# Latent attention's inputs: latent sums and sine inside the projection, rotations between the query units, keys and values in two loads

## What is computed

```
proj = h @ w_in                                   # 1024 -> 384 + 256 + 64
cq, ckv, k_rope = split(proj, [384, 640])
q  = (rmsnorm(cq, g_q)   @ w_q_up ).reshape(B, S, 8, 128 + 64)
kv = (rmsnorm(ckv, g_kv) @ w_kv_up).reshape(B, S, 8, 128 + 128)
q_rope, k_rope = apply_rope(q_rope, cos, sin), apply_rope(k_rope, cos, sin)
s = (q_nope @ k_nope.T + q_rope @ k_rope.T) * scale      # causal softmax, then @ v
```

## Time and profile before

| | us |
|---|---|
| median of three runs | 3182.15 |
| their lowest and highest | 3175.34 and 3193.03 |
| the profiled execution | 3190.56 |
| its span in the trace | 3188.1 |

### The profile page before, as it was taken

One profiled execution on the slowest core, in us unless ns is written; L12 is line 12 of the kernel. 1 busy time (PEld: TensorE's weight loads), 2 busy tenths in 40 slices (PEclk: granted clock), 3 DMA queues, 4 the chain that ended last, 5 costly groups with the idle time before them and its releaser, 6 DMA issues.

```text
span 3188.1 us, 26936 instructions
## 1 busy us (share of the span) xinstructions
PE 2737.7 (86%) x8901; PEld 1634.9 (51%) x8901; DVE 1407.4 (44%) x3069; ACT 624.7 (20%) x1276; POOL 1870.1 (59%) x1393
## 2 busy tenths in 40 slices
PE   8998998777777777777787999899999858899998
PEld 7644443332233223333233476678877534678877
DVE  6747466666666666666414302431111336221111
ACT  2211212121111111111122111321100213121101
POOL 5205666767776777677758770346554482355653
PEclk9999999989998899999999899899999978899999
DMA  6338999999999999999954341022322340123222
GB/s 194 106 111 326 385 365 377 409 400 409 409 409 389 409 409 409 393 409 409 409 202 146 130 133 53 27 79 94 103 86 94 93 156 14 40 79 105 92 91 81
DMA packets 304627, 720.39 MB, mean 226 GB/s; under 512 B 24916, under 2 KB 162050, under 8 KB 304530
## 3 DMA queue, kind: packets, MB, share of 16 engines
q0 software_dynamic: 157248, 574.69, 46.2%
q1 hardware_dynamic: 134802, 131.93, 12.8%
q10 hardware_dynamic: 12480, 12.58, 1.2%
HBM read 717.02 MB, written 2.10 MB: 226 GB/s over the span
## 4 chain that ended last, share of the span: by engine, by line
PE 58%; POOL 14%; DMA 12%; issue 8%; DVE 5%; ACT 2%; SPq 0%; POOLq 0%; DVEq 0%; ACTq 0%
PE ps L881 11%; PE ps L593 10%; PE ps L585 10%; PE ps L589 10%; POOL arena L1263 8%; DMA arena<-in_expert_u_dram,arena 8%; PE ps L846 3%; POOL work L1263 3%; PE ps L979 2%; PE ps L531 2%; PE ps L542 2%; PE ps L794 2%; DMA arena<-in_expert_v_dram,arena 2%; POOL arena L1209 1%; POOL arena L1206 1%
## 5 line engine op out<-in xcount | busy, mean ns | idle before, releaser
L881 PE MATMUL ps<-arena 128*128 128x512 f32 x1536 | 764.7, 644 | 250.0 <-ACT arena L1575 164.6
L881 PEld LDWEIGHTS ps<-arena 128*128 128x128 f32 x1536 | 304.2, 206 | 690.7 <-issue 556.4
L2172 DVE CUSTOM_DVE_ANT_0 arena<-arena,ps 128x1024 f32<-128x1024 f32 x384 | 467.6, 1219 | 306.1 <-DMA arena<-in_expert_u_dram,arena 297.2
L1263 POOL DMA_INDIRECT arena<-in_expert_v_dram,arena x384 | 361.2, 941 | 190.3 <-PE ps L881 100.7
L1263 POOL DMA_INDIRECT arena<-in_expert_u_dram,arena x384 | 361.9, 942 | 149.7 <-issue 100.2
L1236 POOL TENSOR_SCALAR whi_f<-wring 128x2048 fp32r<-128x2048 f32 (+1 forms) x60 | 125.3, 2088 | 317.0 <-DMA wring<-in_ffn_w_in_dram 191.1
L1240 POOL TENSOR_TENSOR wlo<-wring,whi_f 128x2048 fp32r<-128x2048 f32 (+1 forms) x60 | 302.7, 5044 | 11.1 <-POOL whi_f L1236 11.1
L881 PE MATMUL ps<-work,arena 128*128 128x512 f32 x512 | 240.4, 602 | 27.0 <-DMA work<-in_expert_v_dram,arena 27.0
L589 PE MATMUL ps<-n_hi,wlo 128*128 128x512 f32 x1024 | 258.5, 395 | 0.0
L589 PEld LDWEIGHTS ps<-n_hi,wlo 128*128 128x128 f32 x1024 | 195.1, 191 | 43.1 <-issue 1.1
L2355 DVE TENSOR_TENSOR arena<-ps,arena 128x512 f32 x44 | 30.4, 692 | 406.4 <-PE ps L593 406.4
(11 more groups left out here) (307 smaller groups left out, 3698.1 us busy)
## 6 DMA issues: line engine op xcount, KB each, us to landing
wring<-in_ffn_w_in_dram SPq DMA_DIRECT2D x44, 1024.0 KB, 5.0
arena<-in_ada_w_dram POOLq DMA_DIRECT2D x36, 1024.0 KB, 5.9
wring<-in_ffn_w_out_dram SPq DMA_DIRECT2D x16, 1408.0 KB, 6.2
arena<-in_ada_w_dram ACTq DMA_DIRECT2D x12, 1024.0 KB, 6.0
wring<-in_gla_w_in_dram SPq DMA_DIRECT2D x12, 1024.0 KB, 5.2
wring<-in_w_in_dram SPq DMA_DIRECT2D x9, 1024.0 KB, 5.7
wring<-in_w_q_dram SPq DMA_DIRECT2D x8, 1024.0 KB, 10.4
arena<-in_expert_u_dram,arena POOLq DMA_INDIRECT x384, 9.7
```

The lines of the kernel that those rows point to most:

```text
L881: mm = e.matmul(ps[:, 6 + q, :], diag[:, k, :], slot_of(s)[:, q * 512:(q + 1) * 512], start=(n % HEADS == 0 and k == 0), stop=last)
L1263: e.indirect_dma_start(slot_of(seq), None, table, bass.IndirectOffsetOnAxis(ap=idx_flat[:, n * TOPK + k:n * TOPK + k + 1], axis=0)).then_i ...
L2172: inc(e.tensor_tensor_reduce(slot_of(s), slot_of(s), ps[:, 4:6, :].rearrange("p a k -> p (a k)"), 1.0, 0.0, ALU.mult, ALU.add, dots[:, n % ...
```

## The change

ScalarE takes the squares of the five latent chunks out of PSUM next to each copy, into the free tiles `qn`. TensorE sums the first three behind the second projection unit and the other two behind the third. The sine, with its two table loads, stands on ScalarE behind the fourth chunk. The rotary key tile and the four query tiles are rotated inside the query and key units, one behind the second chunk of each query unit and one behind the third key chunk, in banks 6 and 7; VectorE combines them in the order 4, 0, 1, 2, 3. Keys and values come in two loads of four heads (1024 KB each) in place of eight of 256 KB; each load gives four key chunks and four value chunks, a value chunk now being 128 tokens by four heads' 128 columns, taken as a strided slice of the weights. GpSimd's `ada(3)` waits for `norm_full` 6 instead of 5. The counters of chunks are adjusted (eight units become two).

```diff
@@ SP
-            units(IN["mla_w_kv_up_2"][0], 0, 8, 2)
+            for u in range(2):
+                unit(IN["mla_w_kv_up_2"][0], u * 4 * (NOPE + VDIM), 2, width=4 * (NOPE + VDIM), chunks=8)
@@ TensorE, split_linear
-                    for x in lands:
+                    for i, x in enumerate(lands):
                         one(x)
+                        if i in after:
+                            after[i]()
@@ TensorE, latent attention
-            split_linear("mla_in", 3, whi_m, n_hi, n_lo, act, operand(), lands=(16, 16, 32))
-            squares(3, 4)
-            squares(2, 5)
+            def latent_sums(first, n, bank):
+                for k in range(n):
+                    need("sq_ready", c["sq_ready"].at + 1)
+                    mm = e.matmul(ps[:, bank, :], ones[:], qn[:, first + k, :], start=(k == 0), stop=(k == n - 1))
+                inc(mm, "ms_ready")
+
+            def rotate(i):
+                r = (4, 0, 1, 2, 3)[i]
+                if i >= 2:
+                    need("rope_read", i - 1)
+                mm = e.matmul(ps[:, 6 + i % 2, :], rotm[:], cT6[:, 5, :] if r == 4 else qr[:, r, :], start=True, stop=True)
+                inc(mm, "rot_done")
+
+            split_linear("mla_in", 3, whi_m, n_hi, n_lo, act, operand(), lands=(16, 16, 32),
+                         after={1: lambda: latent_sums(0, 3, 4), 2: lambda: latent_sums(3, 2, 5)})
+            base = 2 * (st["u"] % 2)
             need("norm_full", 5)
-            settle()
             for m in range(4):
                 w = slot(3, width=384, n=64)
                 for j in range(3):
                     e.wait_ge(act.sem, act.value(3))
...
                     inc(mm, "chunk_done")
                     act.add()
+                    if j == 1:
+                        e.wait_ge(act.sem, act.value(2))
+                        rotate(m)
             need("norm_full", 6)
+            for u in range(2):
+                w = slot(2, width=4 * (NOPE + VDIM))
+                for i in range(8):
+                    bank = ps[:, (base + 8 * u + i) % 4, :]
+                    e.wait_ge(act.sem, act.value(3))
+                    for k in range(2):
+                        if i < 4:
+                            at = i * (NOPE + VDIM)
+                            mm = e.matmul(bank, w[:, k, at:at + NOPE], cT6[:, 3 + k, :], start=(k == 0), stop=(k == 1))
+                        else:
+                            t = i - 4
+                            values = w[:, k, :].rearrange("p (h c) -> p h c", c=NOPE + VDIM)[:, :, NOPE:NOPE + VDIM]
+                            mm = e.matmul(bank.rearrange("p (h c) -> p h c", c=VDIM), cT6[:, 3 + k, t * P:(t + 1) * P], values,
+                                          start=(k == 0), stop=(k == 1))
+                    inc(mm, "chunk_done")
+                    act.add()
+                    if u == 0 and i == 2:
+                        e.wait_ge(act.sem, act.value(3))
+                        rotate(4)
             settle()
-            def kv_unit():
...
-            pairs_of(MLA_H, kv_unit, act)
-            settle()
-            for r in range(5):
...
             need("rope_ready", 5)
             settle()
@@ GpSimd
-            e.wait_ge(S["norm_full"], 5)
+            e.wait_ge(S["norm_full"], 6)
             ada(3)
@@ ScalarE
-            units(3, copy_to(cT6))
-            e.wait_ge(evacs.sem, evacs.value())
-            squares([cT6[:, k, :] for k in range(3)])
-            root(384)
-            squares([cT6[:, 3 + k, :] for k in range(2)])
-            root(256, bank=5)
...
+            def latent(i):
+                bank = ps[:, 2 * ((st["u"] + i // 2) % 2) + i % 2, :]
+                done.add()
+                e.wait_ge(done.sem, done.value())
+                if i < 5:
+                    inc(e.activation(qn[:, i, :], bank, ACT.Square), "sq_ready")
+                e.activation(cT6[:, i, :], bank, ACT.Copy).then_inc(evacs.sem, 1)
+                evacs.add()
+
+            for i in range(4):
+                latent(i)
             need("angle_ready", 1)
             inc(e.activation(tri, rtmp, ACT.Sin), "trig_ready")
             roots_next()
+            root(384)
+            latent(4)
+            latent(5)
+            root(256, bank=5)
...
@@ VectorE
-            e.wait_ge(S["act_evac"], st["act"] + 6)
             rms(cT6, cT6, lambda k: col("mla_g_q_2", k), 3)
             rms(cT6[:, 3:5, :], cT6[:, 3:5, :], lambda k: col("mla_g_kv_2", k), 2, bank=5)
-            e.wait_ge(S["act_evac"], st["act"] + 6 + 12 + 16)
             need("trig_ready", 1)
-            for r in range(5):
+            for i, r in enumerate((4, 0, 1, 2, 3)):
                 x = cT6[:, 5, :] if r == 4 else qr[:, r, :]
-                need("rot_done", r + 1)
-                own(e.tensor_tensor(rtmp[:, 0, :], ps[:, 4 + r % 4, :], tri[:, 1, :], ALU.mult), "rope_read")
+                need("rot_done", i + 1)
+                own(e.tensor_tensor(rtmp[:, 0, :], ps[:, 6 + i % 2, :], tri[:, 1, :], ALU.mult), "rope_read")
                 own(e.tensor_tensor(x, x, tri[:, 0, :], ALU.mult))
                 own(e.tensor_tensor(x, x, rtmp[:, 0, :], ALU.add), "rope_ready")
```

More of the change, by code:

```diff
@@ L596, in split_products, with split_linear @@
                         between()
-            def split_linear(name, n, high, hi, lo, evac, ready=None, lands=None):
+            def split_linear(name, n, high, hi, lo, evac, ready=None, lands=None, after=None):
                 settle()
@@ L1060, in _ @@
                     for k in range(3):
-                        mm = e.matmul(ps[:, (3 * m + j) % 4, :], w[:, k, j * P:(j + 1) * P], cT6[:, k, :], start=(k == 0), stop=(k == 2))
+                        mm = e.matmul(ps[:, (base + 3 * m + j) % 4, :], w[:, k, j * P:(j + 1) * P], cT6[:, k, :],
+                                      start=(k == 0), stop=(k == 2))
                     inc(mm, "chunk_done")
                     act.add()
+                    if j == 1:
+                        e.wait_ge(act.sem, act.value(2))
+                        rotate(m)
@@ L1769, in _, with up @@
             roots_next()
+            root(384)
+            latent(4)
+            latent(5)
+            root(256, bank=5)
+            st["u"] += 3
+            base = 2 * (st["u"] % 2)
+            def up(i, dst):
+                done.add()
+                e.wait_ge(done.sem, done.value())
+                e.activation(dst, ps[:, (base + i) % 4, :], ACT.Copy).then_inc(evacs.sem, 1)
+                evacs.add()
+            for m in range(4):
+                for j in range(3):
+                    up(3 * m + j, qr[:, m, :] if j == 2 else qn[:, 2 * m + j, :])
+            for u in range(2):
+                for i in range(8):
+                    up(8 * u + i, kn[:, 4 * u + i, :] if i < 4 else vt[:, i - 4, u * 4 * VDIM:(u + 1) * 4 * VDIM])
+            st["u"] += 4 + 2
             SCALE = float(NOPE + ROPE) ** -0.5
@@ L2438, in _ @@
             low_out(MLA_H - 1)
-            skip(3 + 4 + 8)
+            skip(3 + 4 + 2)
             modulation(3)
-            done.add(4)
+            done.add(16)
             residual(gate=48 + 16)
```

## The result

Eight runs of the changed kernel had a median of 3155.65 us (3153.18 to 3161.43) beside 3186.38 us (3171.22 to 3193.03) for eight runs of the kernel before: ratio 0.9915, with an interval of 0.9896 to 0.9933. It is faster: the ratio puts it at about 27 us, and the two medians lie 30.7 apart. The forecast was 3135; its range, 3116 to 3158, holds the time.

A forecast was written before the change was run, and what follows sets the result against it. TensorE was the bound but stood still in handovers before attention. Scores 44.7 us earlier plus 16.1 on the first head, less 14 of contention, gave 46.8: 3143.8 from the profiled 3190.56, or 3135 against the median 8.4 lower; range 3116 to 3158.

The forecast's parts named there:

- The string in front of attention: Handovers from the last projection unit to the first scores: scores start at 2582.8 instead of 2627.5, 44.7 us earlier.
- nothing between ends 0 and 14: Value chunks in the key and value stage: strided weight slices cost 0 us extra, bounds 0 and 14 us.
- No wait for the two loads: Key and value weights in two 1024 KB loads: 0 us of waiting taken, bounds 0 and 3.
- The 10.9 us for keys and values: Key and value stage: 28.4 us against 39.3, 10.9 gained, nearly all of it the missing DMA waits.
- The stalls: Attention beside GpSimd: stalled scaling of probabilities exposes 2.4 us a head over five heads, 12 us, ends 7 and 25.
- The clock: TensorE in attention: clock dips follow the longest stalls, costing 2 us, ends 0 and 6.
- A sign that the prediction had named for being wrong: Attention: the prediction would be wrong if heads beside GpSimd take over 15 us.
- The first head: First head of attention: with the idle gone the clock stays up, 14.5 us instead of 30.6, 16.1 gained.
- The last head: End of attention: the last head was counted at 9.6 us.
- the contention: Attention beside GpSimd: stalls of 12 us and clock dips of 2 give back 14 us, 7 to 31.
- The one that gave 3152: Rival in attention: VectorE becomes the bound, stalls reach TensorE and dips follow; 31 us given back, gain 30; chance 0.17.
- The slower case: TensorE in attention: clock stays down, 7.9 us more a head, slower from 7.7 half-rate heads on, up to 3210; chance 0.02.

The follow-up runs named there:

- the last experiment: Exponentials left in PSUM and the unread matmul, both put on the kernel before, without the change: 3178.34 us, ratio 0.9983.
- the run that removes it: Changed kernel with GpSimd's modulation made to wait until attention is over: 3371.29 us in one run; attention 89.1 us.
- both attention edits: Changed kernel with exponentials left in PSUM and an unread matmul before the third division of each head and second of the first: 3134.32 us, ratio 0.9855.
- the shortened division: Changed kernel with exponentials left in PSUM, where VectorE's division reads them: 3269.92 us, ratio 0.988, on another chip.
- the first, fourth and seventh experiments: On the changed kernel: GpSimd's modulation behind attention, 3371.29 us; rotations back behind the last value chunk, 3302.45 us; eight key and value loads again, 3157.31 us.
- the fourth experiment: Changed kernel with its five rotations put back behind the last value chunk: 3302.45 us, ratio 0.9983, on another chip.

## Why the prediction was right about the direction and wrong about the size

**The string in front of attention** was right, by its steps. From the end of the second unit to the query chunks: 15.5 us foreseen, 15.4 measured. Query stage 34.3 and 34.4. Keys and values with the last copy 29.1 and 29.4. In all 78.9 and 79.2; 44.7 us earlier, and 44.6. The sine started at 2503.22 beside the third unit and nobody waited for it. A rotation's arithmetic was done before its bank was wanted again: VectorE spent at most 0.69, 3.15 and 2.72 us on one, and no wait of TensorE names it. The strided value chunks took 6.87 us for 16 instructions, 0.43 each, as the keys: nothing between ends 0 and 14 was right. No wait for the two loads. GpSimd's call ran from 2519.31 to 2643.68, 124.4 us, as before.

**The 10.9 us for keys and values** came, but not for the reason given. "Nearly all of it the missing DMA waits" is 6.9 us by the earlier trace rows; the other 4 are products at half rate behind those waits (3.31 us in place of 1.72; TensorE was busy 32.4 us of the stretch, and its products take 28.2 at full rate). With eight loads put back in the changed kernel 3.4 us came back, so the number of loads carries only a third of it. It isn't one unlucky execution of the kernel before either: in the last experiment, where this stretch is as before, the same three units wait (2.27, 1.27 and 2.85 us). The loads took 4.0 us to land in the kernel before, 3.8 in that one, and 2.8 in the changed kernel with eight loads. That kernel also has no loops around these units on TensorE and ScalarE, and a rotation among them; what shortened the waits wasn't tried by itself.

**The stalls** were right: 12 us taken (7 to 25), 10.6 measured (idle 21.7 of 113.1 us and 11.1 of 89.1).

**The clock was the step that failed**: "such dips will follow the longest stalls; I take 2 us, ends 0 and 6". It was 13.4 us, over twice the upper end, and it followed more than the longest stalls. The prediction read one idle of 2.30 us with slow products behind it and took only gaps of that size as able to do it. In the changed kernel the clock fell behind stalls of 4.33, 2.87 and 2.52 us, as foreseen, but also in the fifth and sixth heads, behind ordinary gaps of 1.11 and 1.15 us with GpSimd silent, while waits of 2.37 and 1.88 us in the second and fourth heads had full rate behind them. Six clean heads in the earlier trace rows looked like a proof that ordinary gaps are harmless; they were not. A sign that the prediction had named for being wrong came true: heads beside GpSimd "over 15 us". The fourth took 16.7. (A small slip that changes nothing: two table loads and the sine are 3.6 us, not 3.7.)

**The first head** was the second miss: 14.5 us taken without GpSimd, 19.7 measured in the run that removes it. The idle of 28 us is gone, but the pipeline of attention has a gap of its own at its start (1.06 us in that run), and a half-rate stretch follows. With both attention edits, the extra matmul in that gap among them, the first head takes 17.4 at a clock of 1.00. The last head took 8.4 instead of 9.6. Together 4.0 us too low, and with the contention at 24.0 instead of 14, the 13.9 by which attention exceeded the 99.2 of the forecast.

**The execution.** By the profiled ones it is 3153.37 against 3143.8, 9.6 too high: the 13.9 of attention, less the 3.1 by which the second unit happened to end earlier, and about 1 in small pieces. The other 11 of the 20.7 between 3135 and the median lie in which executions these were: 8.4 since the profiled one of before was a long one whose gain was subtracted from a shorter median, 2.3 since the profiled one after was a short one. The stretch that the change removes is itself a part of that scatter: from the third unit to the scores it was 123.8 us in the first trace of before, and 115.7 in the kernel before with attention's edits, where that stretch is untouched; 7.6 of the 8.1 us are TensorE's wait for the rotations, 27.7 and 20.1. Two traces, perhaps of two chips, don't say how much of this is scatter on one chip.

**The rivals.** The one that gave 3152 (VectorE the bound, with dips) was near in size, 31 given back beside the 24.0 and 4.0 measured, and had its dips; but VectorE was not the bound: it was busy 10.95 us of the 16.7 of the slowest middle head beside GpSimd, and 6.67 in a head of 13.4 without it. That 3152 lies near the time is luck in part. The slower case had the clock as its mechanism too, but one that stays down: it needed 7.7 half-rate heads, and the extra TensorE work of 13.4 us, at 9.0 for a whole half-rate head, is one and a half of them.

## What to carry to other kernels

When a stage is moved earlier, cost what it will lie beside, and cost it twice: the stalls, and the clock behind TensorE's gaps, long or short; a clean stretch at full clock in the trace of before doesn't say how near it is to falling. Where a chain leaves one short gap per round on TensorE, an unread matmul in front of the wait can keep the clock up: alone it took attention from about 113 us to 99.5, the shortened division alone to 111.2, and only both together to 88.9, what it takes without GpSimd (89.1). In the time of the whole, only both together stand clear of the changed kernel. And subtract a gain read from one trace only from that trace's own time: a stretch that waits on contended engines can differ by 8 us between two traces.

## What the runs showed of the hardware that was not expected

The same gap doesn't always have the same effect. In one trace of the changed kernel, with GpSimd silent, a wait of 1.11 us in the fifth head was followed by products at half rate, and one of 1.14 us at the same place of the seventh was not. The rows stand in this order:

```profile
2650.81 0.80 PE L1127 MATMUL ps<-ident,arena 128*128 128x128 f32 x3 [1.11 <-DVE arena L2452]
2651.41 1.49 PE L1116 MATMUL ps<-arena 128*128 128x384 f32 x2
```

```profile
2677.61 0.55 PE L1127 MATMUL ps<-ident,arena 128*128 128x128 f32 x3 [1.14 <-DVE arena L2452]
2677.99 0.81 PE L1116 MATMUL ps<-arena 128*128 128x384 f32 x2
```

Over the traces of the kernel before, the changed kernel (two), and the first, fourth and seventh experiments, 27 such gaps of 1.11 to 1.15 us lie in heads beside a silent GpSimd; behind 4 of them the clock fell, two in the changed kernel and two in the fourth experiment. Windows of the changed kernel show what one such fall costs. From 2651.0 to 2658.0 TensorE is busy all 7.00 us at 0.51, some 3.4 us more than at full rate, and the head is 3.2 us longer than a clean one:

```profile
2647.60:2651.00 3.40, 2.29 (x13) 1.32 (x12) 2.23 (x7) 2.17 (x7) 0.00 (x0) 1.00 0.01 2
2651.00:2658.00 7.00, 7.00 (x15) 2.99 (x14) 2.78 (x10) 2.11 (x6) 0.00 (x0) 0.51 0.00 0
```

TensorE was never idle in the low stretch. What decides between the two cases stays open. The length of the gap alone doesn't: 2.23 us left the clock up and 0.99 did not, in one trace of the changed kernel. Its place in time may; no run held the gap fixed and moved only its place. The page "TensorE: Matmul & The Clock Gate" of the Trainium skill tells in its section "A second HAM failure mode: psum-queue depth-cycling" of a kernel whose short idles between groups of matmuls made the clock swing between its two rates. The heads of 13.6 us, with a gap of 1.34 us and a clock of 0.75, agree with that.
